# Aligned dense operands, an earlier Hyena filter layer and a third conditioning weight buffer in a two-layer hybrid backbone step

## The reference

```python
def _trunk_layer(x, mod, lp, gla_s0, rw_s0, grid):
    sh1, sc1, gt1, sh2, sc2, gt2, sh3, sc3, gt3 = [mod[:, j, None, :] for j in range(N_MOD)]
    h = _rmsnorm(x, lp['ffn1_norm']) * (1.0 + sc1) + sh1
    x = x + 0.5 * gt1 * _swiglu(h, lp['ffn1_w_in'], lp['ffn1_w_out'])
    h = _rmsnorm(x, lp['mix_norm']) * (1.0 + sc2) + sh2
    m, s_gla, s_rw = _token_mix(h, lp, gla_s0, rw_s0, grid)
    x = x + gt2 * m
    h = _rmsnorm(x, lp['ffn2_norm']) * (1.0 + sc3) + sh3
    x = x + 0.5 * gt3 * _swiglu(h, lp['ffn2_w_in'], lp['ffn2_w_out'])
    return x, s_gla, s_rw

def _hyena_filter(seq_len, lp):        # z: positions and 32 sinusoids of them
    h = jnp.sin(lp['hy_freq'][0] * (z @ lp['hy_w1'] + lp['hy_b1']))
    h = jnp.sin(lp['hy_freq'][1] * (h @ lp['hy_w2'] + lp['hy_b2']))
    h = (h @ lp['hy_w3']).astype(jnp.float32)
    ...
```

## Time and profile before

| | us |
|---|---|
| median of 3 runs (lowest, highest) | 2038.73 (2037.68, 2042.44) |
| the profiled execution | 2038.66 |
| its span, first to last instruction | 2036.9 |
| TensorE busy | 1909.0 (94%) |
| VectorE busy | 1098.0 (54%) |
| ScalarE busy | 739.0 (36%) |
| mean share of the DMA engines | 38% |
| mean granted TensorE clock | 0.961 |

### The profile page before, as it was taken

How to read it: one execution, slowest core, us unless ns; L and a number is a source line. 1 busy time by engine, 2 the same in 40 slices (tenths; PEclk the granted TensorE clock), 3 DMA queues, 4 the chain that set the end, 5 groups by cost and what they waited for, 6 DMA issues and landing times. The chain is left out here.

```text
span 2036.9 us, 38668 instructions
## 1 busy us (share of the span) xinstructions
PE 1909.0 (94%) x16360; PEld 1749.0 (86%) x16360; DVE 1098.0 (54%) x1845; ACT 739.0 (36%) x1108; POOL 33.0 (2%) x62
## 2 busy tenths in 40 slices
PE   5999999998888989999999999999978798999997
PEld 2888999896555879999999999989757497999997
DVE  3544444765637466555455554476564656655533
ACT  3333333336233244333343333344431424433322
POOL 0000000000001000000000000000000100000000
PEclk8999999998989999999999999999869798999999
DMA  7766233423536233333343333442240401333332
GB/s 263 263 222 221 95 128 137 153 101 111 164 92 208 86 131 127 123 124 107 128 145 124 123 119 119 134 168 86 84 148 4 160 12 66 125 124 124 105 128 88
DMA packets 73193, 263.25 MB, mean 129 GB/s; under 512 B 9697, under 2 KB 10849, under 8 KB 56929
## 3 DMA queue, kind: packets, MB, share of 16 engines
q1 hardware_dynamic: 73056, 261.27, 37.8%
HBM read 259.08 MB, written 2.16 MB: 128 GB/s over the span
## 5 line engine op out<-in xcount | busy, mean ns | idle before, releaser
L156 PE MATMUL ps<-h_head,w_head 128*128 128x386 f32 x1824 | 624.1, 342 | 9.2 <-DVEq L241 4.1
L156 PE MATMUL ps<-h_rest,w_head 128*128 128x386 f32 x1824 | 620.9, 340 | 0.0
L156 PE MATMUL ps<-h_head,w_rest 128*128 128x386 f32 x1824 | 620.0, 340 | 0.0
L217 ACT ACTIVATE w_head<-w_raw 128x2048 fp32r<-128x2048 f32 (+1 forms) x176 | 302.7, 1720 | 607.5 <-PE ps L156 597.3
L220 DVE TENSOR_TENSOR w_rest<-w_raw,w_head 128x2048 fp32r<-128x2048 f32 (+1 forms) x176 | 360.7, 2050 | 212.3 <-ACT w_head L217 212.3
L156 PEld LDWEIGHTS ps<-h_head,w_head 128*128 128x128 f32 x1824 | 346.2, 190 | 28.7 <-issue 18.7
L156 PEld LDWEIGHTS ps<-h_rest,w_head 128*128 128x128 f32 x1824 | 346.4, 190 | 0.2
L156 PEld LDWEIGHTS ps<-h_head,w_rest 128*128 128x128 f32 x1824 | 346.0, 190 | 0.0
L156 PE MATMUL ps<-gu_head,w_head 128*128 128x384 f32 x832 | 281.9, 339 | 11.4 <-DVE gu_rest L808 11.4
L156 PE MATMUL ps<-gu_rest,w_head 128*128 128x384 f32 x832 | 281.6, 338 | 0.0
L156 PE MATMUL ps<-gu_head,w_rest 128*128 128x384 f32 x832 | 281.4, 338 | 0.0
(11 more groups left out here) (294 smaller groups left out, 1786.6 us busy)
## 6 DMA issues: line engine op xcount, KB each, us to landing
w_raw<-in_w_in SPq DMA_DIRECT2D x88, 1024.0 KB, 4.8
w_raw<-in_ada_w SPq DMA_DIRECT2D x48, 1024.0 KB, 6.2
w_raw<-in_w_out SPq DMA_DIRECT2D x64, 704.0 KB, 4.0
w_raw<-in_mix_in SPq DMA_DIRECT2D x26, 1024.0 KB, 4.9
ada_raw<-in_ada_w SPq DMA_DIRECT2D x24, 1024.0 KB, 6.2
w_raw<-in_mix_out SPq DMA_DIRECT2D x8, 1024.0 KB, 4.9
hyena_const<-in_hconst SPq DMA_DIRECT2D x2, 1792.0 KB, 9.5
x<-in_x_in SPq DMA_DIRECT2D x1, 1536.0 KB, 12.0
```

The costliest lines, as they stand in the source:

```text
L156: return nc.tensor.matmul(out, lhsT, rhs, start=start, stop=stop)
L217: return nc.scalar.activation(self.HI[src], self.RAW[src], ACT.Copy)
```

## The change

1. **Addresses.** A 96-byte tensor `EDGE` is allocated first at the top, and the rows of `h_head` and `h_rest` get a pitch of 416 elements (1664 = 13 x 128 bytes), of which 386 are used. All of `w_raw`, `w_head`, `w_rest`, and every row of `h_head` and `h_rest`, then start at a multiple of 128 bytes.
2. **Hyena.** `filter_layer(1)` moves from ahead of unit 2 into unit 1 (second tile, before block `kt` = 4). `turns(1)` moves from n = 2 to n = 1, ahead of that step's convolution; `turns(2)` stays at n = 3. The loads of `HW` and of the positions are written ahead of the loop and that of the remaining constants at n = 2; as units 0 to 2 load nothing there, the queue's order is the same. `EV` shrinks from four rows to two, so that from n = 1 on VectorE waits, before it scales unit n, until ScalarE has taken unit n - 1 out of `EV`.
3. **Conditioning.** In `two_pairs_stage` `Ada` gets three slots, the third a buffer of its own (`ada_raw`, 8 KB a partition). `load_next` waits for the last user of each `w_raw` slot: in layer 0 slot 1 is refilled after unit 14 of 16 used (instead of slot 0 after 15), and slot 0 after the 16th. In layer 1 the order stays. In the feed-forward stage the conditioning row buffer shrinks from two to one.

```diff
+H_ROW = 416
+        EDGE = right(stack, "edge", [128, 24])
         RAW = right(stack, "w_raw", [128, 2, 2048])
...
-                tuple(right(scope, name, [128, KT, WIDE], F32R) for name in ("h_head", "h_rest"))
+                tuple(right(scope, name, [128, KT, H_ROW], F32R)[:, :, 0:WIDE] for name in ("h_head", "h_rest"))
...
-                self.RAW = [RAW[:, s, :] for s in range(slots)] if raw is None else raw
+                self.RAW = [RAW[:, s, :] for s in range(2)] + [sb(scope, "ada_raw", [128, ADA_J * ADA_W])[:, :] for _ in range(slots - 2)] if raw is None else raw
...
-                for u, (src, cols) in enumerate(sources):
-                    sp.wait_ge(self.used, KT * self.sets - 1 + u)
-                    load_ahead(sp, u, cols, src)
+                last_of = [max(u for u in range(KT * self.sets) if u % self.slots == slot) for slot in range(2)]
+                for slot in sorted(range(2), key=lambda slot: last_of[slot]):
+                    src, cols = sources[slot]
+                    sp.wait_ge(self.used, last_of[slot] + 1)
+                    load_ahead(sp, slot, cols, src)
...
-                    ADA = Ada(scope, SEMS[23:28], 2, [4, 6], 2, [...])
+                    ADA = Ada(scope, SEMS[23:28], 2, [4, 6], 1, [...])
...
-                EV = sb(scope, "p_scaled", [128, 4, WIDE])
+                EV = sb(scope, "p_scaled", [128, 2, WIDE])
...
+                    pos = HCONST["pos"][0]
+                    sp.dma_start(HW[:, :], rows(hy_w, lay)).then_inc(hload_done, 16)
+                    sp.dma_start(HC[:, pos:], hconst[:, pos:]).then_inc(hload_done, 16)
                     for n, u in enumerate(UNITS):
                         W.load(sp, n, 2, 0, rows(mix_in, lay * N_MIX + u), 2048)
-                        if n == 1:
-                            ...
+                        if n == 2:
                             sp.dma_start(HC[:, :pos], hconst[:, :pos]).then_inc(hconst_done, 16)
...
+                        if n:
+                            dve.wait_ge(pb_done, n)
                         for t in range(2):
-                            if n >= 2:
-                                dve.wait_ge(pb_done, n - 1)
-                            R.times(EV[:, 2 * (n % 2) + t, :], 2 * (n % 2) + t).then_inc(evict_done, 1)
+                            R.times(EV[:, t, :], 2 * (n % 2) + t).then_inc(evict_done, 1)
...
-                        if n == 2:
-                            turns(1)
-                        if n == 3:
-                            turns(2)
+                        if n in (1, 3):
+                            turns((n + 1) // 2)
...
-                        if n in (2, 3, 5):
+                        if n in (3, 5):
                             filter_layer((n + 1) // 2)
...
                             for kt in range(KT):
+                                if (n, t, kt) == (1, 1, KT // 2):
+                                    filter_layer(1)
...
-                ADA = Ada(scope, SEMS[10:15], 2, [7] * sets, 1, None, mod_row)
+                ADA = Ada(scope, SEMS[10:16], 3, [7] * sets, 1, None, mod_row)
```

More of the change, by code:

```diff
@@ L416, in loaded_unit @@
                 else:
-                    pe.wait_ge(self.raw_full[u % self.slots], 16 * (u // self.slots))
+                    loads = u // self.slots if u % self.slots < 2 else u // self.slots + 1
+                    pe.wait_ge(self.raw_full[u % self.slots], 16 * loads)
             def products(self, pe, n):
@@ L668, in ffn_stage @@
                 if ada_sets:
-                    ADA = Ada(scope, SEMS[23:28], 2, [4, 6], 2, [sb(scope, "ada_raw", [128, KT // 2 * ADA_W])[:, :] for _ in range(2)])
+                    ADA = Ada(scope, SEMS[23:28], 2, [4, 6], 1, [sb(scope, "ada_raw", [128, KT // 2 * ADA_W])[:, :] for _ in range(2)])
                 def in_pairs(eng, body, first=1):
@@ L1001, in mix_in_stage @@
             AC = Steps("sin1 sin2 spec_h0 spec_h1 zt")
-            DV = Steps("c0 d0 e0 a1 n1 m1 r1 s1 t1 clip1 c1 c2 d1 d2 e1 e2 a2 n2 m2 r2 s2 t2 clip2 c3 c4 d3 d4 e3 e4 c5 d5 e5 z w0 w1 filt "
+            DV = Steps("a1 n1 m1 r1 s1 t1 clip1 c0 d0 e0 c1 c2 d1 d2 e1 e2 a2 n2 m2 r2 s2 t2 clip2 c3 c4 d3 d4 e3 e4 c5 d5 e5 z w0 w1 filt "
                        "pa0 pb0 pc0 pd0 y0 pa1 pb1 pc1 pd1 y1 yb out")
@@ L1036, in _ @@
                 def _(sp):
+                    pos = HCONST["pos"][0]
+                    sp.dma_start(HW[:, :], rows(hy_w, lay)).then_inc(hload_done, 16)
+                    sp.dma_start(HC[:, pos:], hconst[:, pos:]).then_inc(hload_done, 16)
                     for n, u in enumerate(UNITS):
                         W.load(sp, n, 2, 0, rows(mix_in, lay * N_MIX + u), 2048)
-                        if n == 1:
-                            pos = HCONST["pos"][0]
-                            sp.dma_start(HW[:, :], rows(hy_w, lay)).then_inc(hload_done, 16)
-                            sp.dma_start(HC[:, pos:], hconst[:, pos:]).then_inc(hload_done, 16)
+                        if n == 2:
                             sp.dma_start(HC[:, :pos], hconst[:, :pos]).then_inc(hconst_done, 16)
@@ L1054, in evict @@
                         for t in range(2):
-                            ps = EV[:, 2 * (n % 2) + t, :]
+                            ps = EV[:, t, :]
                             act.wait_ge(evict_done, 2 * n + t + 1)
@@ L2478, in two_pairs_stage @@
                 mod_row = PR[:, 0:2 * NP - 2:NP, 0:ADA_W // 2].unsqueeze(1)
-                ADA = Ada(scope, SEMS[10:15], 2, [7] * sets, 1, None, mod_row)
-                bias_done = SEMS[15]
+                ADA = Ada(scope, SEMS[10:16], 3, [7] * sets, 1, None, mod_row)
+                bias_done = SEMS[16]
                 def ada_products(pe, s, kt):
```

## The result

The changed kernel takes 2028.56 us (median of 4 runs, 2024.50 to 2031.76) against 2039.28 for the kernel before (4 runs): ratio 0.9944, 95% interval 0.9923 to 0.9966. A second set of runs gave 2029.62 against 2040.07, ratio 0.9940 [0.9922, 0.9958]. The gain is 11 us where 26.5 were forecast. The profiled execution took 2029.15 us with a span of 2027.2, 9.7 us less than the span of before.

What follows compares the result with a forecast made beforehand. TensorE, busy 1909.0 of 2036.9 us, was taken as the bound. Addresses 14.8, Hyena 6.0 and conditioning 5.7 summed to 26.5 us off 2038.66, so 2012 us was predicted, with the range 1999 to 2031.

Steps and rivals of the forecast that it cites:

- I take for a moved product the `gu` rate plus its 2 columns, 174.0 ns: Dense products on h: aligned rows go from 176.7 to 174.0 ns, saving 14.8 us over 5,472 products.
- Rival 1: Dense products on h: addresses change nothing, the rate depends on 386 against 384 columns; 2027 us, chance 0.14.
- Rival 3: Dense products on h: aligned rows pay for their 8-byte tail, 180 to 190 ns; 2045 to 2100 us, chance 0.09.
- The 520 ns of row 4: Timeline of h: three products, 173 ns each, where head and rest start at multiples of 64; evidence that alignment helps.
- The 190 ns behind the rest product of row 0: Timeline of h: a start-to-start distance (84.95 to 85.14) taken as evidence that the distance depends on the row.
- The 16-byte lines: Skill rule on SBUF rows: 97 lines touched before and after, so nothing saved; the prediction left it out of the sum.
- Each link: Hyena, layer 0: filter layer at 359.5 us, unit 3's split done at 369.3, Sin at 369.6; both layers' pauses go, 4.5 us.
- The half-clock slice: Hyena, layer 0, 374.80 to 378.20 us: clock 0.50 behind the pause, counted as gone, 1.5 us.
- the pause: Hyena: TensorE waits for the first Sin, at the second filter layer, 2.1 us in layer 0 and 2.4 in layer 1.
- The refill: End of two_pairs_stage, layer 0: slot 0 loaded at about 718.4 us, landed by 723.7, wanted at 725.64; hidden by 1.9 us.
- the single waits: two_pairs_stage: TensorE's waits for conditioning weights, 6.9 and 6.4 us by layer, of which 5.7 us were counted.

Runs made afterwards that it cites:

- edit 1 alone: Address change, with the smaller EV and conditioning row buffer it needs, against the kernel before: 2040.41 against 2042.85 us, ratio 0.9991.
- edit 3 alone: Third conditioning slot in two_pairs_stage, with load_next by a slot's last use, against the kernel before: 2030.08 us, ratio 0.9941.

## Why the prediction was wrong

**Edit 1, forecast 14.8 us, measured none.** The step that failed is "I take for a moved product the `gu` rate plus its 2 columns, 174.0 ns". `gu` was the only aligned operand of the dense products, and also the only one whose rows end on a multiple of 128 bytes. I priced the 2 columns by their length, 0.9 ns, where they cost 5.7 ns on aligned rows at the pitch of `gu` (173.3 to 179.0), 3.4 in the aligned rows at the pitch of the change (173.3 to 176.7), and 1.4 on unaligned ones (175.3 to 176.7). What alignment gave to 384 columns, 2.0 ns (175.3 to 173.3), went again with the dearer two columns, 3.4 instead of 1.4. Rival 1 is what happened to the time, near its 2027 us, though its reason, the column count alone, is not the whole one. Rival 3, the tail, is nearer to what the rows show; pitch 416 doesn't show its full price, which pitch 448 does: 180.0 ns would have been 5,472 x 3.3 = 18 us slower. That the two effects came out even to 0.01 ns in the kernel (176.67 before and after) is not explained.

The evidence against rival 1 was misread. The 520 ns of row 4 are 527 in the trace's own nanoseconds (171, 173 and 183), against 530 for three mean products. Start times shown at 10 ns steps can't carry a claim of 3 ns a product over three products. The 190 ns behind the rest product of row 0 are 186. And an uneven pattern within one tile does not mean that its dear members can be made cheap: in before, in the changed kernel and 16 bytes on the pattern differs each time and the mean is 176.67 ns each time.

The 16-byte lines of "SBUF — State Buffer" in the Trainium skill, Specifications (TRN2), gave the right result for the kernel, nothing saved. They don't give the size of what was measured beside it: rows at pitches of 416 and 448 touch the same 97 lines and take 176.7 and 180.0 ns.

**Edit 2, forecast 6.0 us, measured 6.3** (3.78 and 2.53 by the stretches). Each link held: the filter layer at 358.2 us (forecast 359.5) with its load landed, the split of unit 3 at 368.0 (369.3), the Sin at 368.4 (369.6). All are some 1.3 us early because the whole stretch began 1.3 us earlier, at 340.87 instead of 342.21. The half-clock slice counted at 1.5 us belongs to the pause: where the pause is left in (edit 1 alone, edit 3 alone) the mixing input of layer 0 runs at a clock of 0.98 and takes 142.6 and 142.4 us; in the seven profiles without the pause it is 1.00 and 137.0 to 137.2.

**Edit 3, forecast 5.7 us, measured 5.9** (2.8 and 3.1), and 6.9 alone. The refill stayed hidden. The layers came out more even than the 3.3 and 2.4 forecast, so the sum is closer than its parts: they miss by 0.5 and 0.7 us in opposite directions. No run separates the single waits, so which of them counted in full stays as forecast, not as shown.

**A term that the sum did not have: +5.1 us between the two profiled executions.** The sum had nothing for `gla_and_pair_stage`, whose code is unchanged. Its time moved by +6.7 and -1.6 us with the granted clock. The kernel before had happened to have its layer 0 at 0.88 in the profiled execution. No edit accounts for the 5.1 us: the kernel with all three edits and the rows 16 bytes on took 116.54 us in layer 0, at 0.88. They are chance of the executions that were profiled and no part of the miss by the medians, whose gain of 11 us is what edits 2 and 3 should give, 12.2 us by their stretches, within the runs' own spread. The miss is edit 1.

## What to carry to other kernels

An operand from which a rate is borrowed must agree in every property that could set it; here start and end of a row changed together, and a row of matmuls by itself tells them apart. In a stretch of short products the clock is part of its time: compare such stretches at equal granted clock, over several executions, before a microsecond in them is given to an edit. And a wait that goes is not worth its length: a third slot gave 5.9 us for 13.3 us of waits in `two_pairs_stage`, and 10.1 us for 15.0 in the first stretch, where the clock rose with it.

## What the runs showed of the hardware

A product of 384 columns whose rows start and end at multiples of 128 bytes took 173.33 ns at all four distances tried between the operands; every other layout tried with the kernel's weight buffers, 384 unaligned or 386 columns, took 175.0 to 180.0. With these buffers a pitch of 448 or 512 elements made nearly every 386-column product take 180 ns, where pitch 416 gave 171 to 183 in a fixed pattern with a mean of 176.7. With weights 4 KB apart the same 384 aligned columns took 175.6 and 386 at pitch 448 took 176.6, so the place of the weights counts too. If the two shift columns of `h` could be computed elsewhere at no cost, aligned rows at a pitch of 384 would save 5,472 x (176.7 - 173.3) = 19 us; this is an estimate from the two measured distances and was not tried.

Two things stay open: what in the addresses sets the pattern, and what decides how long the clock stays at 1.2 GHz in the first mixer stretch, where filling 1.8 of 3.1 us at its border changed nothing that can be told and fewer waits inside it went with 0.01 more of mean clock.
